# Two small matrix products of a two-block transformer kernel: one after the other, or matmul by matmul in two halves of the array

## What is computed

```python
def compress_tokens(kv, w1, w2, pe):
    bsz, seq = kv.shape[:2]
    n_cmp = (seq - CMP_BLOCK) // CMP_STRIDE + 1            # 15 windows
    idx = np.arange(n_cmp)[:, None] * CMP_STRIDE + np.arange(CMP_BLOCK)[None, :]
    blocks = kv[:, idx] + pe[None, None, :, None, :]
    flat = jnp.swapaxes(blocks, 2, 3).reshape(bsz, n_cmp, ATT_KV_HEADS, CMP_BLOCK * ATT_HEAD_DIM)
    return jax.nn.silu(flat @ w1) @ w2
...
    k_cmp = compress_tokens(kc, cmp_w1_k, cmp_w2_k, cmp_pe_k)
    v_cmp = compress_tokens(vc, cmp_w1_v, cmp_w2_v, cmp_pe_v)
```

## Time and profile before

| | us |
|---|---|
| median of 3 runs (2505.35 to 2508.05) | 2507.85 |
| the profiled execution, its own time | 2508.06 |
| its span in the profile | 2506.3 |
| TensorE busy | 2473.7 (99%) |
| VectorE busy | 1455.4 (58%) |
| ScalarE busy | 1251.8 (50%) |
| mean granted TensorE clock | 0.994 of full |

### The profile page before, as it was taken

One profiled execution on the slowest core, in us unless ns is written; L12 is line 12 of the kernel. 1 busy time (PEld: TensorE's weight loads), 2 busy tenths in 40 slices (PEclk: granted clock), 3 DMA queues, 4 the chain that ended last, 5 costly groups with the idle time before them and its releaser, 6 DMA issues.

```text
span 2506.3 us, 32631 instructions
## 1 busy us (share of the span) xinstructions
PE 2473.7 (99%) x11947; PEld 2067.1 (82%) x11947; DVE 1455.4 (58%) x1732; ACT 1251.8 (50%) x1604; POOL 44.9 (2%) x103
## 2 busy tenths in 40 slices
PE   8999999999999999999999999999999999999997
PEld 7888878888888888888888888878888888888886
DVE  6479665545445454445566566566666666544465
ACT  5357744444444444444654355456556555444464
POOL 2300000000000000000000000000000000000000
PEclk9999999999999999999999999999999999999999
DMA  7543445666666666555654555555565656665554
GB/s 254 175 134 113 135 136 184 191 187 191 186 191 188 189 192 202 192 192 178 171 175 135 151 143 177 186 158 183 186 185 183 190 178 189 199 200 193 193 194 142
DMA packets 234754, 446.27 MB, mean 178 GB/s; under 512 B 14288, under 2 KB 31012, under 8 KB 234144
## 3 DMA queue, kind: packets, MB, share of 16 engines
q1 hardware_dynamic: 231920, 434.83, 56.2%
q0 software_dynamic: 2736, 10.10, 1.3%
HBM read 442.78 MB, written 2.10 MB: 178 GB/s over the span
## 4 chain that ended last, share of the span: by engine, by line
PE 96%; DVE 2%; ACT 1%; issue 0%; DMA 0%; SPq 0%; DVEq 0%; ACTq 0%
PE pg L2191 26%; PE pg L2193 26%; PE pg L2192 26%; PE pg L2250 3%; PE pg L2251 3%; PE pg L2252 3%; PE pt L2851 1%; DVE wlo L1347 1%; PE pt L2666 1%; PE pt L2262 1%; PE pt L2370 1%; PE pt L2435 1%; PE pt L2461 1%; PE pt L2448 0%; PE pt L2649 0%
## 5 line engine op out<-in xcount | busy, mean ns | idle before, releaser
L1347 DVE TENSOR_TENSOR wlo<-raw,whi 128x1024 fp32r<-128x1024 f32 (+3 forms) x844 | 1004.9, 1197 | 980.4 <-ACT whi L653 978.7
L653 ACT ACTIVATE whi<-raw 128x1024 fp32r<-128x1024 f32 (+3 forms) x844 | 871.8, 1036 | 1164.1 <-PE pg L2193 1048.5
L2191 PE MATMUL pg<-whi,AH 128*128 128x512 f32 (+1 forms) x1920 | 749.5, 390 | 5.1 <-DVE AL L1486 3.0
L2193 PE MATMUL pg<-whi,AL 128*128 128x512 f32 (+1 forms) x1920 | 742.8, 387 | 0.0
L2192 PE MATMUL pg<-wlo,AH 128*128 128x512 f32 (+1 forms) x1920 | 742.1, 387 | 0.0
L2191 PEld LDWEIGHTS pg<-whi,AH 128*128 128x128 f32 x1920 | 362.1, 189 | 77.1 <-DVE AL L1486 3.4
L2193 PEld LDWEIGHTS pg<-whi,AL 128*128 128x128 f32 x1920 | 361.6, 188 | 73.7
L2192 PEld LDWEIGHTS pg<-wlo,AH 128*128 128x128 f32 x1920 | 362.3, 189 | 70.8
L2191 PE MATMUL pg<-whi,FH 128*128 128x512 f32 x696 | 271.3, 390 | 0.0
L2193 PE MATMUL pg<-whi,FL 128*128 128x512 f32 x696 | 270.8, 389 | 0.0
L2192 PE MATMUL pg<-wlo,FH 128*128 128x512 f32 x696 | 270.8, 389 | 0.0
(11 more groups left out here) (477 smaller groups left out, 2033.1 us busy)
## 6 DMA issues: line engine op xcount, KB each, us to landing
raw<-w_up SPq DMA_DIRECT2D x264, 512.0 KB, 3.8
raw<-w_down SPq DMA_DIRECT2D x176, 512.0 KB, 3.6
raw<-w_in SPq DMA_DIRECT2D x152, 512.0 KB, 3.6
raw<-w_gate SPq DMA_DIRECT2D x88, 512.0 KB, 3.6
raw<-w_out SPq DMA_DIRECT2D x64, 512.0 KB, 3.6
raw<-w_ple_gate SPq DMA_DIRECT2D x32, 512.0 KB, 4.5
raw<-w_in SPq DMA_DIRECT2D x32, 388.0 KB, 3.2
raw<-w_in SPq DMA_DIRECT2D x16, 280.0 KB, 3.0
```

What stands on the lines that cost most here:

```text
L653: A(whi[:, n % RING, 0:w], raw[:, n % RING, 0:w], ACT.Copy).then_inc(hi_ready, 1)
L1347: V.tensor_tensor(wlo[:, n % RING, 0:w], raw[:, n % RING, 0:w], whi[:, n % RING, 0:w].bitcast(F32), ALU.subtract).then_inc(lo_ready, 1)
L2191: mm(o, xh, wh, start=first and k == 0, stop=False)
L2193: ins = mm(o, xl, wh, start=False, stop=last and k == SK - 1)
```

## The change

The values no longer follow the keys. One function `hidden()`, called ahead of step 29, alternates the matmuls: a key matmul into partitions 0 to 59, then the value matmul of the same k into partitions 64 to 123, of the same columns 0 to 255 of bank 0. Nothing is inserted ahead of step 28. `HT_` is half as wide and holds keys at partitions 0 to 59 and values at 64 to 123, so `hid_silu` is two activations of 60 x 256. `hid_turn` takes the value transposes from partitions 64 to 123 and writes them to bank 0 (the keys' go to bank 1 as before); `hid_out` reads them there. The number of matmuls and transposes, their sizes and the places of everything else stay.

```diff
-        HT_ = at("HT_", [P, 2 * CMP_HID], F32, o_x)
+        HT_ = at("HT_", [P, CMP_HID], F32, o_x)
...
             def hid_silu():
                 act.wait_ge(hid_sum, 1)
-                A(HT_[0:60, :], pt[0:60, 0, :], ACT.Silu).then_inc(hid_act, 1)
+                A(HT_[0:60, :], pt[0:60, 0, 0:CMP_HID], ACT.Silu)
+                A(HT_[64:124, :], pt[64:124, 0, 0:CMP_HID], ACT.Silu).then_inc(hid_act, 1)
 
             def hid_out():
                 act.wait_ge(hid_turned, 1)
-                hid = pt[:, 1, 0:256].rearrange("p (b c) -> p b c", c=64)
-                A(HK[:], hid[:, 0:2, 0:60], ACT.Copy).then_inc(hid_act, 1)
+                hid_k, hid_v = (pt[:, b, 0:P].rearrange("p (m c) -> p m c", c=64) for b in (1, 0))
+                A(HK[:], hid_k[:, :, 0:60], ACT.Copy).then_inc(hid_act, 1)
...
-            def hidden(i):
-                if i == 0:
-                    pe.wait_ge(cmpw_landed, 16 * 11)
-                    pe.wait_ge(q_out, 2)
-                w, x = ((W1K, KFK), (W1V, KFV))[i]
+            def hidden():
+
+                pe.wait_ge(cmpw_landed, 16 * 11)
+                pe.wait_ge(q_out, 2)
                 for k in range(KT):
-                    ins = mm(pt[0:60, 0, i * CMP_HID:(i + 1) * CMP_HID], x[:, k, :], w[:, k, :], start=k == 0, stop=k == KT - 1)
-                if i:
-                    ins.then_inc(hid_sum, 1)
+                    mm(pt[0:60, 0, 0:CMP_HID], KFK[:, k, :], W1K[:, k, :], start=k == 0, stop=k == KT - 1)
+                    ins = mm(pt[64:124, 0, 0:CMP_HID], KFV[:, k, :], W1V[:, k, :], start=k == 0, stop=k == KT - 1)
+                ins.then_inc(hid_sum, 1)
 
             def hid_turn():
                 pe.wait_ge(hid_act, 1)
                 for i in range(4):
-                    ins = tr(pt[:, 1, i * 64:i * 64 + 60], HT_[0:60, i * P:(i + 1) * P], C[0:60, 0:60])
+                    r = slice(64 * (i // 2), 64 * (i // 2) + 60)
+                    ins = tr(pt[:, 1 - i // 2, (i % 2) * 64:(i % 2) * 64 + 60], HT_[r, (i % 2) * P:(i % 2 + 1) * P], C[r, r])
...
-                if n in (28, 29):
-                    hidden(n - 28)
+                if n == 29:
+                    hidden()
```

More of the change, by code:

```diff
@@ L826, in hid_out @@
                     for h in range(NKV):
-                        x = hid[:, 2 + m, h * NCMP:(h + 1) * NCMP].unsqueeze(1).to_broadcast([P, 4, NCMP])
+                        x = hid_v[:, m, h * NCMP:(h + 1) * NCMP].unsqueeze(1).to_broadcast([P, 4, NCMP])
                         ins = A(HV[:, m, h, :, 0:NCMP], x, ACT.Copy)
```

## The result

| | before | changed | |
|---|---|---|---|
| first comparison, median (lowest to highest), 7 runs each | 2505.41 (2502.68 to 2508.35) | 2496.85 (2495.07 to 2500.72) | ratio 0.9970, 95% interval 0.9959 to 0.9980 |
| second comparison, 15 and 9 runs | 2505.30 (2502.67 to 2508.55) | 2498.07 (2494.86 to 2500.69) | ratio 0.9973, 95% interval 0.9963 to 0.9983 |
| the profiled executions, own time | 2508.06 | 2500.18 | 7.88 less |
| their spans | 2506.3 | 2498.4 | 7.9 less |

The changed kernel is 0.27 to 0.30% faster, 7 to 8 us.

A forecast was written before the change was run, and what follows sets the result against it. The prediction took TensorE, busy 99% of the span, as the bound. The pairs save 7.24 us, all other terms zero: 2507.85 - 7.24 = 2500.6 us, range 2497.4 to 2503.8.

The forecast's parts named there:

- What bounds: Whole kernel: TensorE, busy 99% of the span, sets the time; shortening its queue shortens the kernel.
- The pairs: Inserted block on TensorE: a key and a value record together take one record's 0.217 us; saves 7.24 us.
- Rival A: Inserted block: the key and value matmuls don't overlap, saving only 0.28 us, time 2507.6; chance 0.05, half overlap included.
- Rival B: Inserted block: stationary loads no longer hidden behind matmuls, each record 0.217 + 0.133 us, time 2516.1; chance 0.03.
- hid_silu: ScalarE activation split in two: at most 0.4 us more, covered by later slack, so zero.
- hid_turn: Four TensorE transposes, two from partitions 64 to 123: gain up to 0.1 us or lose 0.15, taken as zero.
- The wait ahead of the pairs: TensorE ahead of step 29: the eleven loads and q_out, waited for 12 matmuls later, cost zero.
- the ring: Four slots filled by the splits: one pause of 8.11 us fills them all, so the lead stays; zero.
- k_turn(0): TensorE step moved from 111.22 to 104.0 us; slack behind its GpSimd copies shrinks from 15.7 to 8.5; zero.
- Rival C: Behind the block: a load or copy not tied to TensorE takes the gain back; half back gives 2504.2; chance 0.04.
- D, the clock: TensorE's half-clock stretches, 3.2 us each: one more gives 2503.8, chance 0.07; one less 2497.4, chance 0.05.

The follow-up runs named there:

- e3: Changed kernel with two key matmuls, then two value matmuls, and so on, instead of strict alternation; block 7.10 us, one execution of 2500.63 us.
- e5: Changed kernel with eight key matmuls, then eight value matmuls, and so on; block 11.52 us, one execution of 2505.80 us.
- e2: Changed kernel, still alternating, but both products on partitions 0 to 59, values in bank 1; block 13.95 us, one execution of 2504.96 us.
- e4: Changed kernel with four key matmuls, then four value matmuls, and so on; block 8.29 us, one execution of 2495.57 us.
- e1: Changed kernel with all 16 key matmuls before all 16 value matmuls; block 13.14 us, 2501.29 us against 2508.22 of before, ratio 0.9979.

## Why the prediction was right, and where not

- **What bounds:** right. The 7.22 us gained by 112 us are still gained at 2493.
- **The pairs:** right, and the term was exact: 7.24 for the block with its way in and out was forecast from L2461, 7.50 - 0.26 = 7.24 was measured. New operands on both sides and 60 columns instead of 64 cost nothing. The reason given was too narrow. The prediction asked whether neighbours in the queue overlap; e3 to e5 show that they need not be neighbours, up to four records apart.
- **Rival A** (no overlap) did not come; e2, which puts both products in one half, has the 64 x 0.216 that it was priced at (64 x 0.217). The 2507.6 itself was not met: the one execution of e2 took 2504.96, with one stretch at half clock fewer.
- **Rival B** (the loads come out) did not come, not even in e2, where rows and columns are the same and the operands change after each matmul: the loads of 0.13 lie in the 0.216 of matmuls on all 128 rows. The rule of the Trainium skill ("TensorE: Matmul & The Clock Gate", What overlaps and what doesn't), that a load runs beside a matmul only when its row group differs, does not hold here. The estimate of 5.4 us from the Trainium skill's figure for three column tiles (the same page, Measured speedup vs the span model) was also too low for this kernel; the pairs take 0.216, not 0.27.
- **`hid_silu`:** 0.29 more on ScalarE, within the bound of 0.4, and no one waited. **`hid_turn`:** taken as zero, gained 0.12 to 0.13, a little over the bound of 0.1: four transposes on two row halves overlap in part, and the same four on one half, in e2, gain nothing. That term was mis-sized by 0.1.
- **The wait ahead of the pairs, the ring, `k_turn(0)`:** zero, as forecast; TensorE is busy for 244.99 of the 245 us from 80 to 325.

```profile
80.00:325.00 245.00, 244.99 (x1577) 209.56 (x1576) 171.21 (x278) 156.69 (x338) 20.70 (x51) 1.00 0.47 134
```

- **Rival C** (given back later) did not come.
- **D, the clock:** the price was right at the place, 3.2 a stretch (2.8 at the end of the kernel, by the groups), and the number was not. The prediction let one come or go, with chances of 0.07 and 0.05. But nine of the sixteen executions of the changed kernel had a mean clock above 0.994, and profiled executions have up to two stretches fewer. That is the main reason why the first median, 2496.85, lies 0.5 below the end of the range (2497.4); 0.1 from the transposes and some 0.5 from the early rise of the clock, which the prediction did not have, add to it. The profiled execution, with the three stretches of before, took 2500.18 against 2500.8 forecast for it. The step that failed is that the base was taken as one number: the sum was made against an execution in the highest group (2508.06), and the median of three runs shown (2507.85) was in it as well, while the medians of before in the later series are 2505.41 (7 runs), 2508.22 (13) and 2505.30 (15), by the share of the groups in each. With the last as base and 7.24 the second median, 2498.07, is met to 0.01, but that is luck: the two series mix the groups in different shares, the first comparison gives 8.56, and at equal clock the difference is 7.9.

## What to carry to other kernels

Here a float32 matmul with 60 columns of the array costs as much per moving column as one with all 128 (0.216 for 256; the eight whole-array records of 128 in the earlier trace rows take 1.04 with the 0.27 of the last one, so they start 0.11 apart). Two of them, put to partitions 0 and 64 and not more than four records apart in TensorE's queue, cost as much as one. Only 128 rows, a moving length of 256 and float32 were tried. If the kernel has such a pair somewhere already, the distance of its starts is the price, and no estimate is needed. Where an effect of a few us is to be judged, first sort the executions of both kernels by what the clock did, and compare within a group.

## What the runs showed of the hardware

- The two column halves start their records independently, out of program order, with a look-ahead of four records (two float32 matmuls): a record starts once its half is free and the record four places ahead of it has started. Seen at every change of half in groups of 8, 16 and 32 records, which are 4, 8 and 16 matmuls (e4, e5, e1), and consistent with pairs and groups of 2.
- When a half gets going again, its first distance of starts is 0.26 to 0.27 instead of 0.216, 0.05 more (93.29 to 93.55 in the changed kernel). In groups of 2 (e3) one such distance comes without a pause ahead of it.
- TensorE's clock fell to half for 6.8 us in one to three places of the kernel from profile to profile. Each of the first two was worth 3.2 us at its place, with the same waits of TensorE ahead of it (0.8 and 1.4 us) whether it came or not. And the clock rose to full for the first time between some 14 and 17 us from the start, worth up to 1.2 us between executions. The executions of one kernel thereby spread over 6 us (2502.67 to 2508.66, and 2494.86 to 2500.72), nearly as much as the whole effect of this change.
